# A chain of fp32r matmuls on one core: its SBUF buffers placed anew, X and the phase buffers at the low end, the weight buffers at the upper end

## What is computed

```python
# first block
h = x + mamba2_mixer(rms_norm(x, g0), ...)      # in: 1024 -> 5152, scan of 32 heads, out: 2048 -> 1024
k_nope, k_rope, v = mla_shared_kv(h, ...)       # down: 1024 -> 288, rms_norm, up: 256 -> 2048
h = h + mla_mixer(rms_norm(h, g1), ...)         # in: 1024 -> 1408, q up: 384 -> 1536, 16 heads, out: 1024 -> 1024
x = rms_norm(h, g_final)
# second block
x = x + 0.5 * swiglu(rmsnorm(x, n1), w_in, w_out)     # 1024 -> 2 * 2816, 2816 -> 1024
x = x + hybrid_mixer(rmsnorm(x, nm), ...)             # in: 1024 -> 7168, two projections, out: 1024 -> 1024
x = x + 0.5 * swiglu(rmsnorm(x, n2), w_in, w_out)
return rmsnorm(x, final_norm)
```

## Time and profile before

| | us |
|---|---|
| median of three executions | 1914.16 |
| lowest, highest | 1909.27, 1915.06 |
| the profiled execution, its own time | 1911.54 |
| its span (first to last instruction) | 1909.5 |
| PE (matmuls) busy in it | 1850.4 |
| PEld (weight loads) busy | 1464.7 |
| DVE busy | 1042.0 |
| ACT busy | 737.8 |
| POOL busy | 38.6 |

### The profile page before, as it was taken

The page is one execution under the profiler, slowest core; times in us unless marked ns, Lnnn a source line. Parts: engine busy times, 40 slices in busy tenths (PEclk is TensorE's granted clock), DMA queues, the critical chain, the costliest instruction groups (busy, mean ns, idle before and its releaser), DMA issues.

```text
span 1909.5 us, 20718 instructions
## 1 busy us (share of the span) xinstructions
PE 1850.4 (97%) x8312; PEld 1464.7 (77%) x8312; DVE 1042.0 (55%) x1484; ACT 737.8 (39%) x1205; POOL 38.6 (2%) x114
## 2 busy tenths in 40 slices
PE   6899999999999899999999999999999999999997
PEld 5677777877866578888888878888888888888885
DVE  6888876565477656454433336554443555444233
ACT  4577766333456643222222243222222332222221
POOL 2000101100000000000000000000000000000000
PEclk9999999999999999999999999999999999999998
DMA  4221212222210022322333322222222222222331
GB/s 147 71 72 63 71 67 74 92 80 98 89 45 24 22 89 90 105 93 100 94 92 93 131 78 81 97 100 100 95 93 100 88 96 93 99 100 90 98 91 53
DMA packets 47038, 164.58 MB, mean 86 GB/s; under 512 B 5216, under 2 KB 5472, under 8 KB 46944
## 3 DMA queue, kind: packets, MB, share of 16 engines
q1 hardware_dynamic: 46656, 163.07, 25.5%
q10 hardware_dynamic: 288, 0.20, 0.0%
HBM read 161.15 MB, written 2.10 MB: 85 GB/s over the span
## 4 chain that ended last, share of the span: by engine, by line
PE 82%; DVE 10%; ACT 4%; issue 2%; POOL 0%; DMA 0%; SPq 0%; DVEq 0%; ACTq 0%; POOLq 0%
PE pb L656 25%; PE pb L658 25%; PE pb L657 25%; PE pb L741 1%; DVE wl L1291 1%; DVE st L1660 1%; ACT wr L1005 1%; PE pb L946 1%; PE pb L947 1%; PE pb L948 1%; ACT PP L1180 1%; DVE XL L1309 1%; DVE CV L1444 1%; DVE LL L1528 1%; DVE QT L1631 1%
## 5 line engine op out<-in xcount | busy, mean ns | idle before, releaser
L656 PE MATMUL pb<-XR,wr 128*128 128x512 f32 x1592 | 633.2, 398 | 19.6 <-DVE XL L1309 9.1
L657 PE MATMUL pb<-XL,wr 128*128 128x512 f32 x1592 | 622.9, 391 | 0.0
L658 PE MATMUL pb<-XR,wl 128*128 128x512 f32 x1592 | 622.4, 391 | 0.0
L1291 DVE TENSOR_TENSOR wl<-raw,wr 128x1024 fp32r<-128x1024 f32 (+1 forms) x306 | 369.5, 1208 | 424.4 <-ACT wr L1005 424.2
L1005 ACT ACTIVATE wr<-raw 128x1024 fp32r<-128x1024 f32 (+1 forms) x306 | 317.6, 1039 | 275.5 <-PE pb L658 249.6
L656 PEld LDWEIGHTS pb<-XR,wr 128*128 128x128 f32 x1592 | 300.7, 189 | 94.3 <-issue 22.5
L658 PEld LDWEIGHTS pb<-XR,wl 128*128 128x128 f32 x1592 | 300.3, 189 | 64.1
L657 PEld LDWEIGHTS pb<-XL,wr 128*128 128x128 f32 x1592 | 301.0, 189 | 60.1
L1014 ACT ACTIVATE SQ<-H 128x512 f32<-128x512 f32 x42 | 26.5, 632 | 134.2 <-DVE H L1455 63.5
L658 PE MATMUL pb<-ffn1HR,wl 128*128 128x512 f32 x176 | 70.2, 399 | 0.0
L658 PE MATMUL pb<-ffn2HR,wl 128*128 128x512 f32 x176 | 70.2, 399 | 0.0
(11 more groups left out here) (303 smaller groups left out, 2233.7 us busy)
## 6 DMA issues: line engine op xcount, KB each, us to landing
raw<-in_ffn_in SPq DMA_DIRECT2D x88, 512.0 KB, 3.2
raw<-in_mix_in SPq DMA_DIRECT2D x48, 512.0 KB, 3.2
raw<-in_ssm_in SPq DMA_DIRECT2D x41, 512.0 KB, 3.2
raw<-in_ffn_out SPq DMA_DIRECT2D x32, 512.0 KB, 3.5
raw<-in_ffn_out SPq DMA_DIRECT2D x16, 384.0 KB, 3.1
raw<-in_mla_in SPq DMA_DIRECT2D x11, 512.0 KB, 3.2
raw<-in_ssm_out_a SPq DMA_DIRECT2D x8, 512.0 KB, 3.2
raw<-in_ssm_out_b SPq DMA_DIRECT2D x8, 512.0 KB, 3.2
```

The source lines that it names most:

```text
L656: e.matmul(o, r, xr, start=first, stop=False)
L657: e.matmul(o, r, xl, start=False, stop=False)
L658: return e.matmul(o, l, xr, start=False, stop=last)
L1291: e.tensor_tensor(wl[j % NS][:, 0:width(j)], raw[j % NR][:, 0:width(j)], wr[j % NS][:, 0:width(j)].bitcast(F32), ALU.subtract).then_inc(s_ ...
```

## The change

Only the allocation of SBUF changes. `nc.sbuf_tensor` gets a side: `left` takes bytes from the low end upwards, as before, `right` from the upper end downwards. XR, XL and all buffers of phases go left, in an order that has the streamed operands first; what lives throughout, and YN and SZ, goes right. The order of instructions, semaphores and DMAs is the same on every engine.

```diff
-    def sb(name, shape, dt=F32, stack=top):
-        return stack.enter_context(nc.sbuf_tensor(name, shape, dt))
+    def sb(name, shape, dt=F32, stack=top, side="right"):
+        return stack.enter_context(nc.sbuf_tensor(name, shape, dt, side=side))
+
+    def low(name, shape, dt, stack):
+        return sb(name, shape, dt, stack, "left")
 
+    XR = low("XR", [128, KT, S], F32R, top)
+    XL = low("XL", [128, KT, S], F32R, top)
     raw = [sb(f"raw{i}", [128, 1024]) for i in range(NR)]
     wr = [sb(f"wr{i}", [128, 1024], F32R) for i in range(NS)]
     wl = [sb(f"wl{i}", [128, 1024], F32R) for i in range(NS)]
-    XR = sb("XR", [128, KT, S], F32R)
-    XL = sb("XL", [128, KT, S], F32R)
     H = sb("H", [128, KT, S])
...
-    YR = sb("YR", [128, 16, S], F32R, ph2)
-    YL = sb("YL", [128, 16, S], F32R, ph2)
+    YR = low("YR", [128, 16, S], F32R, ph2)
+    YL = low("YL", [128, 16, S], F32R, ph2)
...
-    CQ = sb("CQ", [128, 2, 3, S], F32R, ph)
-    CK = sb("CK", [128, 2, 2, S], F32R, ph)
+    CQ = low("CQ", [128, 2, 3, S], F32R, ph)
+    CK = low("CK", [128, 2, 2, S], F32R, ph)
...
-    HRS.append(sb("ffn1HR", [128, FT, S], F32R, ph))
-    HLS.append(sb("ffn1HL", [128, FT, S], F32R, ph))
+    HRS.append(low("ffn1HR", [128, FT, S], F32R, ph))
+    HLS.append(low("ffn1HL", [128, FT, S], F32R, ph))
...
-    YA = sb("YA", [128, 2, 8, S], F32R, ph)
+    YA = low("YA", [128, 2, 8, S], F32R, ph)
...
```

More of the change, by code:

```diff
@@ L307, in build_in @@
     ph2 = ExitStack()
[L308 to L324, removed]
+    LL = [low(f"LL{i}", [128, 2, 1664], F32, ph2) for i in range(2)]
+    BC = low("BC", [128, 2, S], F32, ph2)
@@ new lines, in build_in @@
+    tri = low("tri", [128, S], F32, ph2)
+    pick = low("pick", [64, 32], F32R, ph2)
+    before = low("before", [128, 128], F32, ph2)
+    U = [low(f"U{i}", [128, S + 3], F32, ph2) for i in range(2)]
+    CV = [low(f"CV{i}", [128, S], F32, ph2) for i in range(2)]
+    XD = low("XD", [128, 4, 4, 128], F32, ph2)
+    CB = [low(f"CB{i}", [128, 1280], F32, ph2) for i in range(2)]
+    CH = low("CH", [64, S], F32R, ph2)
+    HQ = low("HQ", [128, 128], F32R, ph2)
+    DT, T1, T2, T3, CM = [low(n, [128, 128], F32, ph2) for n in ("DT", "T1", "T2", "T3", "CM")]
@@ L325, in build_in @@
+    DTT = low("DTT", [128, 4, 32], F32, ph2)
+    NCT = low("NCT", [128, 4, 32], F32, ph2)
+    CMT = low("CMT", [128, 4, 32], F32, ph2)
+    negA = low("negA", [128, 1], F32, ph2)
+    prior = low("prior", [128, 1], F32, ph2)
     ph2.close()
-    YR = sb("YR", [128, 16, S], F32R, ph2)
-    YL = sb("YL", [128, 16, S], F32R, ph2)
+    YR = low("YR", [128, 16, S], F32R, ph2)
+    YL = low("YL", [128, 16, S], F32R, ph2)
     ph2.close()
     ph.close()
-    CQ = sb("CQ", [128, 2, 3, S], F32R, ph)
@@ L342, in build_in @@
-    OT = sb("OT", [128, S], F32, ph)
-    st4 = [sb(f"st4{i}", [128, 4, 4], F32, ph) for i in range(3)]
+    CQ = low("CQ", [128, 2, 3, S], F32R, ph)
+    CK = low("CK", [128, 2, 2, S], F32R, ph)
+    KH = [low(f"KH{i}", [96, S], F32, ph) for i in range(4)]
+    PT = [low(f"PT{i}", [128, 1280], F32, ph) for i in range(2)]
+    PP = [low(f"PP{i}", [128, 1280], F32, ph) for i in range(3)]
+    SG = low("SG", [128, 8, S], F32, ph)
+    VT = low("VT", [128, 4, 1024], F32, ph)
+    QT = [low(f"QT{i}", [96, S], F32, ph) for i in range(4)]
@@ L344, in build_in @@
+    TQ = low("TQ", [128, S], F32, ph)
+    RK = low("RK", [128, S], F32, ph)
+    Q2 = [low(f"Q2{i}", [96, S], F32, ph) for i in range(2)]
+    OT = low("OT", [128, S], F32, ph)
+    st4 = [low(f"st4{i}", [128, 4, 4], F32, ph) for i in range(3)]
     craw = [PP[0][:, 0:512], PP[0][:, 512:1024], PP[1][:, 0:512], PP[1][:, 512:1024], PP[2][:, 0:512]]
@@ L348, in build_in @@
     ph = ExitStack()
-    HRS.append(sb("ffn1HR", [128, FT, S], F32R, ph))
-    HLS.append(sb("ffn1HL", [128, FT, S], F32R, ph))
-    GAS.append([sb(f"ffn1GA{i}", [128, S], F32, ph) for i in range(2)])
-    UPS.append([sb(f"ffn1UP{i}", [128, S], F32, ph) for i in range(2)])
+    HRS.append(low("ffn1HR", [128, FT, S], F32R, ph))
+    HLS.append(low("ffn1HL", [128, FT, S], F32R, ph))
+    GAS.append([low(f"ffn1GA{i}", [128, S], F32, ph) for i in range(2)])
+    UPS.append([low(f"ffn1UP{i}", [128, S], F32, ph) for i in range(2)])
     ph.close()
-    YA = sb("YA", [128, 2, 8, S], F32R, ph)
[L356 to L362, removed]
+    YA = low("YA", [128, 2, 8, S], F32R, ph)
+    VG = low("VG", [128, 4, 1024], F32, ph2)
+    UG = low("UG", [128, 8, S], F32, ph2)
+    BB = low("BB", [128, 1024], F32, ph2)
+    WS = low("WS", [128, 8, 128], F32, ph2)
+    G1 = [low(f"G1{i}", [128, S], F32, ph2) for i in range(3)]
+    vs = low("vs", [128, 4, 2], F32, ph2)
+    vr = low("vr", [128, 4], F32, ph2)
     ph2.close()
-    YB = sb("YB", [128, 2, 8, S], F32R, ph)
-    MG = sb("MG", [128, 2, 8, S], F32R, ph)
+    YB = low("YB", [128, 2, 8, S], F32R, ph)
+    MG = low("MG", [128, 2, 8, S], F32R, ph)
     C1 = TB
-    TP = [sb(f"TP{i}", [128, S + 2], F32, ph) for i in range(2)]
-    CW = [sb("CW", [128, S], F32, ph), ACC]
+    TP = [low(f"TP{i}", [128, S + 2], F32, ph) for i in range(2)]
+    CW = [low("CW", [128, S], F32, ph), ACC]
     ph.close()
[L370 to L373, removed]
+    HRS.append(low("ffn2HR", [128, FT, S], F32R, ph))
+    HLS.append(low("ffn2HL", [128, FT, S], F32R, ph))
+    GAS.append([low(f"ffn2GA{i}", [128, S], F32, ph) for i in range(2)])
+    UPS.append([low(f"ffn2UP{i}", [128, S], F32, ph) for i in range(2)])
     ph.close()
```

## The result

The changed kernel takes 1945.86 us, the median of four executions (1945.14 to 1949.22), against 1911.95 for the kernel before beside it: a ratio of 1.0173 (1.0157 to 1.0189).

The account below looks back on a forecast made before the run. PE's stream of fp32r matmuls was taken as the bound; 31.8 + 1.3 + 0 - 0.5 + 0 - 1 = +31.6 us on 1911.5 gave 1943.1, and with 2.6 for the median 1945 us, range 1932 to 1956.

Parts of the forecast that it names:

- Which operand counts?: From ukv_v beside mix_v: a matmul steps at 226.7 ns only if both operands are low; either one high costs 6.7 ns.
- Item 1: 4776 X matmuls get high stationary weights, +31.8 us; 192 mix_v matmuls get a high moving operand, +1.3 us.
- Item 2: 2208 phase-buffer matmuls: moving operand becomes low, stationary high, so still slow: 0 us, bounds +5.8 and -5.8 us.
- Items 3 and 4: Other fp32 TensorE products moving down, -0.5 us; DVE and ACT work on moved buffers, 0 within +-2 us.
- Item 5: Where PE idles for others, a slower PE shortens the waits: -1 us, at most 2.2 us in the first 100 us.
- The sum: All terms together, +31.6 us on 1911.5, with 2.6 us added for the median: 1945 us, range 1932 to 1956.
- (a): Rival: only the moving operand's place counts, X stays at 226.7 ns; faster, about 1904 us; chance 0.10.
- (b): Rival: no address effect, something else in the stages makes the two levels; stays at 1914 us; chance 0.05.
- (c): Rival: slower still, two high operands cost twice (1951 us) or a third level for high weights; chance 0.10 of 0.85.

Follow-up runs that it names:

- weights-high kernel: The kernel before with wr and wl alone put at the upper end of SBUF, all else sliding down: 1930.01 us against 1915.26, ratio 1.0083.

## Why the prediction was right, and where its reasons were wrong

**The bound and the two levels.** Right as to the bound: PE set the time, and what changed was the step. The two levels, 226.7 and 233.3 ns, were read rightly, but they were the steps of two distances out of at least four: 229.0 and 234.2 ns stand in the map beside them.

**"Which operand counts?"** Wrong, and the main error. Its last sentence, that a matmul steps at 226.7 ns only if both its operands are low, was refuted three times: by both operands high (226.9 ns, 1897.67 us), by the change with 96 bytes of padding, X low and weights high (226.7 ns), and by ffn1HL at 100 to 144 KB with low weights (226.7 ns). What the runs show in its place is that the two start addresses must agree modulo 256 bytes. The pair ukv_v and mix_v was rightly read as "the stationary operand's address counts too", but I took "address" for "height". Every buffer of the slow fp32r products lay behind the 1028-byte `vec`, so its height and its offset were one and the same in it, and the table of places in whole KB hid the offset. An exact address beside each buffer would have shown it before any run.

**Item 1, X and mix_v: +33.1 us.** The mechanism behind it was wrong, and that the step grew by about the right amount was luck: the change happens to give them distances of 160 and 96 bytes instead of 0; with 96 bytes more in front of the weights the same places cost nothing. The size was near: the X step is 234.2 and not 233.3 ns, so 4776 x 7.5 ns = 35.8 and 192 x 6.67 ns = 1.3 us, together 37.1.

**Item 2, the phase buffers: 0.** It asked whether they lie under a border, and there is none. They went from a distance of 96 to one of 160, 0.9 ns a step: 2208 x 0.9 ns = +2.0 us. Both bounds given there (two high operands cost twice, or cost nothing) were about the wrong quantity.

**Items 3 and 4, fp32 products and DVE: -0.5 and 0.** Small, as said. DVE was busy 1041.8 us against 1042.0. The product of LL and XD, now at lower places, has a median duration of 486 ns in both profiles, so no gain shows. Item 4 names ACC, at 92 KB, as a buffer of its row; the row has RS, at 96 to 98 KB, which changes nothing in it.

**Item 5, the waits: -1.** Too small. PE's idle time fell from 59.1 us (1909.5 less 1850.4) to 52.8 (1943.1 less 1890.3), by 6.3 us; 4.5 of them in the first stage (23.2 us down to 18.7), whose waits are spread beyond the first 100 us, on which I had based the bound. PE's busy time grew by 39.9 us, where items 1 to 4 had 31.8 + 1.3 - 0.5 = 32.6. So the matmuls were put 7.3 us too low and the waits absorbed 5.3 us more than said. The two errors nearly cancelled, and 39.9 - 6.3 = 33.6 us, the growth of the span, came out near the 31.6 of the sum. Even the 39.9 is not steps alone: by the measured steps items 1 and 2 make 39.1, up to 3.8 us go with the half clock shown above, and so the matmuls outside steady stretches must have paid less than the full price, which was not followed further.

**The sum.** By its own terms it is 1914.16 + 31.6 = 1945.8 us, not 1945, and the ends of its range are 1933.7 and 1956.5, not 1932 and 1956. The measured 1945.86 us lies within either.

**The rivals.** (a), only the moving operand counts, falls with the weights-high kernel: moving X stayed at 128 modulo 256 and slowed to 234.4 ns. (b), no address effect, falls with 160 bytes of padding worth 16 us. The Trainium skill, TensorE: Matmul & The Clock Gate, in the section on the 56 ns step, gives 216 ns for 512 columns; no steady stretch used here shows less than 226.7. The Trainium skill, SBUF — State Buffer, in Who interferes with whom, lets PE's two read ports wait on nobody; that the step here hangs on how the addresses of the two reads relate sits badly with that, though no run shows where in PE the time is lost. (c), a cost that doubles, did not occur: the slowest steady step seen is 234.4 ns.

**A rival was missing**: that the change makes its loss by an accident of alignment, and not by where it puts things. It would have given the same 1945 us, but another advice: not "move the weights back down", but "add 96 bytes".

## What to carry to other kernels

Where fp32r matmuls stream back to back, give the stationary and the moving buffers start addresses that agree modulo 256 bytes, by padding after odd-sized small tensors: here, with fp32r operands of 128x128 and 128x512, 160 unused bytes gave 0.9% and 96 were worth 45 us. Other forms were not tried. Before reading an address effect from a trace, write down the exact addresses and look at their low bits; two populations that differ in height may differ in alignment too. A time that comes out as forecast does not confirm the mechanism; here one experiment of four runs was enough to overturn it.

## What the runs showed of the hardware

All at a granted clock of 1.00 in the stretches used, 128x512 fp32r, weight loads between all matmuls:

- The steady step is 226.7 ns when the start addresses of the two operands agree modulo 256 bytes, 229.0 at a distance of 64, and 233.3 to 234.4 at 32, 96, 128, 160, 192 and 224. At distance 0 the height of either in SBUF made no difference, from 0 to 208 KB: 226.7 to 226.9 ns with both low, both high, or one of each.
- It holds with the roles changed too: with weights moving, mix_v at distance 0 had 226.7, ukv_v at distance 160 had 233.3 over six steps, and ukv_v at distance 64 had 229.0, with 96 bytes of padding.
- In a stream whose tiles have different distances, the tile at distance 0 took 231.3 ns a step as the mean. The mean over eight equidistant offsets, 232.5 ns, is near the mean of the eight lines of the map, 232.1.
- Why the distance matters, whether through the weight load that runs beside the moving reads or otherwise, was not tried. Nor were bf16 operands, or distances that are no multiple of 32 in a steady stretch. Plain fp32 matmuls were not studied.
